# Feed-forward units whose output products come one unit later in a fused decoder trunk

## The reference

```python
for i in range(2):
    x = x + 0.5 * swiglu_ffn(rms_norm(x, ffn1_norm[i]), ffn1_w_in[i], ffn1_w_out[i])
    x = x + mixer_i(rms_norm(x, mix_norm[i]))     # i = 0: pooling + convolution; i = 1: spatial gating
    x = x + 0.5 * swiglu_ffn(rms_norm(x, ffn2_norm[i]), ffn2_w_in[i], ffn2_w_out[i])
return rms_norm(x, final_norm)

def swiglu_ffn(x, w_in, w_out):                   # w_in (1024, 5632), w_out (2816, 1024)
    gate, up = jnp.split(x @ w_in, 2, axis=-1)
    return (jax.nn.silu(gate) * up) @ w_out
```

## Time and profile before

| | |
|---|---|
| median of three runs | 899.32 us |
| the profiled execution's own time | 900.39 us |
| its span, first to last instruction | 898.6 us |
| mean granted TensorE clock | 0.996 |
| TensorE (PE) busy | 885.0 us |
| weight loads (PEld) busy | 737.6 us |
| VectorE (DVE) busy | 567.7 us |
| ScalarE (ACT) busy | 421.1 us |
| GpSimd (POOL) busy | 57.3 us |
| read from HBM | 168.11 MB |

### The profile page before, as it was taken

The page is one execution under the profiler, slowest core; times in us unless marked ns, Lnnn a source line. Parts: engine busy times, 40 slices in busy tenths (PEclk is TensorE's granted clock), DMA queues, the critical chain, the costliest instruction groups (busy, mean ns, idle before and its releaser), DMA issues.

```text
span 898.6 us, 11277 instructions
## 1 busy us (share of the span) xinstructions
PE 885.0 (98%) x4114; PEld 737.6 (82%) x4114; DVE 567.7 (63%) x595; ACT 421.1 (47%) x470; POOL 57.3 (6%) x60
## 2 busy tenths in 40 slices
PE   8899999999999999999999999999999999999997
PEld 7688888889888888888888888888899878888885
DVE  5666646757957765565566655665678476565653
ACT  7444435448845543444444534444553354443432
POOL 1000000404720000000000000000000000000000
PEclk9999999999999999999999999999999999999999
DMA  8885665643353877597638575675475278567531
GB/s 283 277 273 172 226 223 172 241 160 142 119 163 131 266 243 237 163 301 239 183 121 293 176 244 188 206 246 180 141 281 157 78 238 279 188 218 234 164 129 47
DMA packets 149933, 180.18 MB, mean 201 GB/s; under 512 B 7885, under 2 KB 134377, under 8 KB 149896
## 3 DMA queue, kind: packets, MB, share of 16 engines
q1 hardware_dynamic: 149880, 179.67, 60.9%
q10 hardware_dynamic: 16, 0.00, 0.0%
HBM read 168.11 MB, written 1.05 MB: 188 GB/s over the span
## 4 chain that ended last, share of the span: by engine, by line
PE 92%; DVE 2%; ACT 2%; DMA 2%; issue 1%; POOL 1%; SPq 1%; POOLq 0%; ACTq 0%
PE acc L1244 10%; PE acc L1246 10%; PE acc L1245 10%; PE ga L1244 10%; PE ga L1246 10%; PE ga L1245 10%; PE ub L1246 10%; PE ub L1245 10%; PE ub L1244 10%; PE tp L1306 1%; DMA xs<-xs 1%; DVE w_lo L866 1%; POOL w_lo L521 1%; DMA raw<-in_ffn_w_in_dram 0%; PE ga L1517 0%
## 5 line engine op out<-in xcount | busy, mean ns | idle before, releaser
L866 DVE TENSOR_TENSOR w_lo<-raw,w_hi 128x2048 fp32r<-128x2048 f32 x147 | 333.8, 2297 | 78.1 <-ACT w_hi L561 76.3
L561 ACT ACTIVATE w_hi<-raw 128x2048 fp32r<-128x2048 f32 x151 | 284.2, 1907 | 28.3 <-DMA raw<-in_ffn_w_in_dram 16.3
L1244 PE MATMUL acc<-w_hi,act_hi 128*128 128x512 f32 x416 | 164.3, 395 | 3.8 <-DVE act_lo L1042 3.8
L1246 PE MATMUL acc<-w_hi,act_lo 128*128 128x512 f32 x416 | 162.5, 391 | 0.0
L1245 PE MATMUL acc<-w_lo,act_hi 128*128 128x512 f32 x416 | 162.3, 390 | 0.0
L1244 PE MATMUL ga<-w_hi,xn_hi 128*128 128x512 f32 x384 | 150.8, 393 | 1.5 <-DVE w_lo L950 1.2
L1246 PE MATMUL ga<-w_hi,xn_lo 128*128 128x512 f32 x384 | 149.5, 389 | 0.0
L1244 PE MATMUL ub<-w_hi,xn_hi 128*128 128x512 f32 x384 | 149.5, 389 | 0.0
L1246 PE MATMUL ub<-w_hi,xn_lo 128*128 128x512 f32 x384 | 149.5, 389 | 0.0
L1245 PE MATMUL ga<-w_lo,xn_hi 128*128 128x512 f32 x384 | 149.4, 389 | 0.0
L1245 PE MATMUL ub<-w_lo,xn_hi 128*128 128x512 f32 x384 | 149.4, 389 | 0.0
(11 more groups left out here) (160 smaller groups left out, 652.0 us busy)
## 6 DMA issues: line engine op xcount, KB each, us to landing
raw<-in_ffn_w_in_dram SPq DMA_DIRECT2D x172, 512.0 KB, 4.9
raw<-in_ffn_w_out_dram SPq DMA_DIRECT2D x88, 512.0 KB, 4.2
xs<-xs SPq DMA_DIRECT2D x160, 64.0 KB, 2.1
raw<-in_sgu_w_in_dram SPq DMA_DIRECT2D x16, 512.0 KB, 4.9
raw<-in_ab_w_in_dram SPq DMA_DIRECT2D x12, 512.0 KB, 5.3
raw<-in_ab_w_out_dram SPq DMA_DIRECT2D x8, 512.0 KB, 4.1
raw<-in_sgu_w_out_dram SPq DMA_DIRECT2D x8, 512.0 KB, 5.7
raw<-in_ffn_w_in_dram SPq DMA_DIRECT2D x8, 256.0 KB, 5.9
```

The lines of the kernel that those rows point to most:

```text
L561: act.activation(w_hi[:, n % RING, :], raw[:, n % RAW, :], ACT.Copy).then_inc(hi_split, 1)
L866: dve.tensor_tensor(w_lo[:, n % RING, :], raw[:, n % RAW, :], w_hi[:, n % RING, :].bitcast(F32), ALU.subtract).then_inc(lo_split, 1)
L1244: pe.matmul(dst, s_hi, m_hi, start=start, stop=False)
L1246: return pe.matmul(dst, s_lo, m_hi, start=False, stop=stop)
```

## The change

Five things are edited.

1. On TensorE an FFN stage runs unit 0, unit 1, unit 2, output of unit 0, unit 3, output of unit 1, ... The outputs of units 8, 9 and 10 stand behind unit 10. The output slab of unit 0 is now slab b + 6; slabs b + 4 and b + 5 are unit 2's.
2. ScalarE, VectorE and SyncE follow that order. `hidden_hi` gets a wait for `slab_used`. `to_turn` of a stage's unit 9 moves from the next stage's first loads to behind its own last load.
3. `norm` on VectorE makes the low part of token tile 0's second half after the additions of token tile 1, and after mixer 1 two slabs are split inside `norm(k, 0)` (`ahead`).
4. `between` is called for each half of the output product, so that the transposes of half 1 come after three more matmuls.
5. Eight more warm-up matmuls, in three groups behind waits, follow the four.

```diff
 # SyncE
+                    for a in range(2):
+                        load_rows(b + 2 + a, w_in, a, pair(WIDTH, FF))
                     def turn(i, run):
                         for j in range(2):
-                            n, s = b + 2 + 3 * j, 1 + j
+                            n, s = b + 4 + 3 * j, 2 + j
                             for a in range(2):
                                 load_rows(n + a, w_in, a, pair(s * WIDTH, FF, i), run)
-                            if j or run is not None:
-                                to_turn(d + s - 1, run)
-                            load_out(n + 2, w_out, bass.ds(i * 4 + 2 * (s - 1), 2), run)
+                            to_turn(d + s - 1, run)
+                            load_out(n + 2, w_out, bass.ds(i * 4 + 2 * j, 2), run)
...
+                        load_rows(n + a, w_in, a, pair((STEPS - 1) * WIDTH, FF))
+                    to_turn(d + STEPS - 2)
                     for s in range(STEPS - 3, STEPS):
-                        if s == STEPS - 2:
-                            to_turn(d + STEPS - 2)
-                        load_out(n, w_out, slice(2 * s, 2 * s + 2))
-                        n += 1
-                    if k + 1 == len(stages):
-                        to_turn(d + TURNS)
+                        load_out(n + s - STEPS + 5, w_out, slice(2 * s, 2 * s + 2))
+                    to_turn(d + TURNS)
 # ScalarE
-            def norm(k, t):
+            def norm(k, t, ahead=0):
...
+                split_to(ahead)
...
-            def hidden_hi(slot, d, i=None):
+            def hidden_hi(slot, n, d, i=None):
+                act.wait_ge(slab_used, at(n, RING, i))
                 act.wait_ge(turn_landed, at(64 * d, 128, i))
...
                     split_to(b + 5)
+                    hidden_hi(0, b + 2, d + 1)
+                    split_to(b + 6)
+                    for t in range(TT):
+                        gate_rows(t, b + 2, r + 1, f + 1, ACT.Silu, scaled=late)
+                    split_to(b + 7)
                     with act.Fori(0, (STEPS - 3) // 2) as i:
                         for j in range(2):
-                            n, s = b + 2 + 3 * j, 1 + j
-                            hidden_hi(j, d + s, i)
+                            n, s = b + 4 + 3 * j, 2 + j
+                            hidden_hi(1 - j, n, d + s, i)
                             split(n + 4, i)
...
+                    n, s = b + 4 + 3 * (STEPS - 3), STEPS - 1
+                    hidden_hi(1, n, d + s)
+                    split_to(n + 4)
+                    for t in range(TT):
+                        gate_rows(t, n, r + s, f + s, ACT.Silu, scaled=late)
+                    last_hi(e // STEPS + 1)
+                    split_to(n + 7)
 # VectorE
+                if t:
+                    norm_lo(k, 0, 1)
                 dve.wait_ge(ms_ready, 4 * k + 2 * t + 2)
...
+                split_to(ahead)
+                norm_lo(k, t, 0)
+                if t:
+                    norm_lo(k, t, 1)
...
                     split_to(b + 5)
+                    hidden_lo(0, e)
+                    split_to(b + 6)
+                    for t in range(TT):
+                        product_rows(t, g + 2, scaled=late)
+                        to_blocks(t, f + 1)
+                    split_to(b + 7)
...
+                    n, s = b + 4 + 3 * (STEPS - 3), STEPS - 1
+                    hidden_lo(1, e + s - 1)
+                    split_to(n + 4)
+                    for t in range(TT):
+                        product_rows(t, g + 2 * s, scaled=late)
+                    last_lo(e + s)
+                    split_to(n + 7)
 # TensorE
             warm_up(WARM_UP)
+            pe.wait_ge(first_hi, 1)
+            warm_up(3)
+            pe.wait_ge(first_lo, 1)
+            warm_up(3)
+            pe.wait_ge(hi_piece, 1)
+            warm_up(2)
...
                     def step(j, start, i=None):
-                        n = b + 2 + 3 * j
-                        unit(n, f + 1 + j, i)
+                        n = b + 4 + 3 * j
+                        unit(n, f + 2 + j, i)
                         step_out(n + 2, j, e + 1 + j, start, i)
+                    unit(b + 2, f + 1)
                     step(0, True)
...
+                    unit(n, f + STEPS - 1)
                     slab_ready(out8)
                     pe.wait_ge(h_done, e + STEPS - 2)
                     slab_out(out8, 0, 0, False, False)
...
                     turned()
-                    slab_out(out8 + 1, 0, 2, False, False, parts=(1,))
-                    slab_out(out8, 1, 0, False, False, parts=(0,))
+                    slab_ready(out8 + 1)
+                    pe.wait_ge(h_done, e + STEPS - 1)
+                    slab_out(out8 + 1, 0, 2, False, False)
                     slab_ready(out8 + 2)
                     pe.wait_ge(h_done, e + STEPS)
                     slab_out(out8 + 2, 0, 4, False, True).then_inc(first_out, 1)
-                    slab_out(out8, 1, 0, False, False, parts=(1,)).then_inc(slab_used, 1)
+                    slab_out(out8, 1, 0, False, False).then_inc(slab_used, 1)
                     slab_out(out8 + 1, 1, 2, False, False).then_inc(slab_used, 1)
-                        slab_out(out8 + 2, 1, 4, False, True, lambda: transposes(k + 1, 0)).then_inc(slab_used, 1)
+                        slab_out(out8 + 2, 1, 4, False, True, lambda h: transposes(k + 1, 0, (h,))).then_inc(slab_used, 1)
```

More of the change, by code:

```diff
@@ L357, in _ @@
                 b, d = base[k], ffn0[k] // STEPS * TURNS
-                after = k > 0 and stages[k - 1][0] == "ffn"
                 if kind == "ffn":
@@ L405, in _ @@
                             .then_inc(mix1_landed, 16)
-                    n = b + 2 + 3 * (STEPS - 3)
+                    n = b + 4 + 3 * (STEPS - 3)
                     for a in range(2):
[L408 to L412, removed]
-                    for s in range(STEPS - 3, STEPS):
-                        if s == STEPS - 2:
-                            to_turn(d + STEPS - 2)
-                        load_out(n, w_out, slice(2 * s, 2 * s + 2))
-                        n += 1
-                    if k + 1 == len(stages):
-                        to_turn(d + TURNS)
+                        load_rows(n + a, w_in, a, pair((STEPS - 1) * WIDTH, FF))
+                    to_turn(d + STEPS - 2)
+                    for s in range(STEPS - 3, STEPS):
+                        load_out(n + s - STEPS + 5, w_out, slice(2 * s, 2 * s + 2))
+                    to_turn(d + TURNS)
                 elif kind == "mix0":
@@ L422, in _ @@
                     for j in range(2):
-                        if j:
-                            to_turn(d)
                         load_rows(b + j, ab_w_in[0], j, pair(gate, a - gate))
@@ L693, in _ @@
                 else:
-                    norm(k, 0)
+                    norm(k, 0, b + 3 if stages[k - 1][0] == "mix1" else 0)
                     split_to(b)
@@ L887, in root_wait, with norm_lo, norm @@
                 dve.wait_ge(rstd_ready, roots)
-            def norm(k, t):
+            def norm_lo(k, t, h):
+                n = small[("norm", k, t, h)]
+                dve.wait_ge(xn_hi_ready, 4 * (k - 1) + 2 * t + h + 1)
+                hi = xn_hi[:, 4 * h:4 * h + 4, t * P:(t + 1) * P]
+                dve.tensor_tensor(xn_lo[:, 4 * h:4 * h + 4, t * P:(t + 1) * P],
+                                  tp[n % 2][:, :].rearrange("p (c t) -> p c t", c=4),
+                                  hi.bitcast(F32), ALU.subtract).then_inc(small_free, 1)
+            def norm(k, t, ahead=0):
                 scale = 0.5 if stages[k - 1][0] == "ffn" else 1.0
@@ L1080, in _ @@
                     split_to(b + 5)
+                    hidden_lo(0, e)
[4 more added lines that the diff above has]
+                    split_to(b + 7)
                     with dve.Fori(0, (STEPS - 3) // 2) as i:
                         for j in range(2):
-                            n, s = b + 2 + 3 * j, 1 + j
-                            hidden_lo(j, e + j, i)
+                            n, s = b + 4 + 3 * j, 2 + j
+                            hidden_lo(1 - j, e + 1 + j, i)
                             split(n + 4, i)
@@ L1279, in slab_out @@
                 for c in parts:
-                    if between is not None and c == 1:
-                        between()
                     for h in range(2):
+                        if between is not None and c == 1:
+                            between(h)
                         o = slice(c * D + h * HALF, c * D + (h + 1) * HALF)
@@ L1416, in tail @@
                             if k + 1 < len(stages):
-                                between = lambda: transposes(k + 1, 0)
+                                between = lambda h: transposes(k + 1, 0, (h,))
                             else:
@@ L1474, in _ @@
                             .then_inc(small_full, 1)
-                    n = b + 2 + 3 * (STEPS - 3)
-                    out8 = n + 4
-                    unit(n, f + STEPS - 2)
```

(7 more changed lines are left out.)

7 lines of the change are left out of this document (1 added, 6 removed).

## The result

The changed kernel takes 919.96 us (median of four runs, 917.49 to 922.19) against 898.52 us for the kernel before on the same chip: the ratio is 1.0235, with a 95% interval of 1.0216 to 1.0255. It is 21 us slower. Forecast were 912.0 us and a range of 905 to 917: the direction and the places are right, the size is not.

What follows compares the result with a forecast made beforehand. TensorE was taken as the bound, busy 885.0 of 898.6 us. Removed waits -7.15, new waits +12.6, clock +4.5, stage ends +2.1 and opening +0.65 made +12.7 us: 912.0 us, range 905 to 917.

Steps and rivals of the forecast that it cites:

- The opposite sign: Rival: unit 2's bank `ga` is free in time, so the kernel gains, 894.9 us; chance 0.10, of which 0.05 below 894.8.
- The rival's condition: For `ga` free at unit 2: a chain from unit 0's blocks to the product of 9.1 us or less, not 11.7.
- Together 12.6 us: New TensorE waits at unit 2's start: 4.1, 3.3, 2.6 and 2.6 us in stages 0, 2, 3 and 5.
- 3 x 1.5 = 4.5 us: Clock falls behind the waits at unit 2: three at 1.5 us each; bounds none and four, 0 to 6.0.
- every wait lowers the clock: Rival: all four waits at unit 2 bring a clock fall, 913.5 us; chance 0.15.
- 0.98 us did not (7.74): In the opening of the kernel before, an idle of 0.98 us was read as bringing no clock fall.
- The end of a stage: Three splits instead of two ahead of `norm`: transposes wait 0.7 us at three stage ends, 2.1 us (0 to 3).
- The opening: Eight more warm-up matmuls at kernel start: first 128x512 matmul near 8.8 us, a delay of 0.65 us (0.3 to 1.2).
- What the change removes: Stage 0's wait 3.45 and slow stretch 1.5, stage 5's waits 1.2, slow transposes 1.0: together 7.15 us.

Runs made afterwards that it cites:

- gates_ahead: Changed kernel with both engines' splits of slab b + 6 moved behind unit 1's gates and products; 896.4 us, 0.9966 of the kernel before.
- order_alone: Changed order of units and outputs with both gates_and_tail edits, but norm, transposes and warm-up as in the kernel before; 894.65 us, 0.9964 of the kernel before.
- gates_and_tail: gates_ahead plus the next stage's first slab split ahead of unit 10's gates; 893.33 us, 0.9932 of the kernel before.
- norm_alone: Kernel before with only the change's norm, `ahead` and transposes by halves; 895.44 us, 0.9969 of the kernel before.
- warm_alone: Kernel before with only the eight more warm-up matmuls added; 898.80 us, 0.9998 of the kernel before.

## Why the prediction was right in place and wrong in size

- *The opposite sign was not in danger.* Unit 2 behind unit 1 waits for unit 1's product, because slab b + 6's split stands ahead of the gates and its load behind `to_turn`. gates_ahead shows it: with that order undone the kernel is 2.6% faster than changed. The rival's condition was too mild, though: a chain of 9.1 us frees the bank in time for stages 3 and 5 only; by the prediction's own distances stage 2 wants 8.4 and stage 0 7.9.
- *"Together 12.6 us"*, the waits at unit 2, was mis-sized: they measured 14.95. The chain from unit 0's blocks to the product was put at 11.7 us (12.0 in stage 0) and is 12.1, 12.9, 12.1 and 12.5 us in stages 2, 3, 5 and 0. The missing part is mostly in the issues: I took 2.9 us from the blocks to the slab's second DMA, and it is 3.2 (stage 5) to 3.9 us (stage 3, where the four turn DMAs take 3.20 us and not 2.49). The first of the slab's two DMAs takes 0.59 us behind the turn's, not the 0.4 I took from another place. Landing was 4.4 for 4.3, and the splits and the product were as forecast. TensorE adds about 0.15 us between product and first matmul, and each restart costs 0.16 us besides the idle (36.50 - 31.63 - 4.48 - 0.23). I counted the restart for the waits removed and left it out for the new ones, 0.65 us over the four.
- *"3 x 1.5 = 4.5 us"*, the clock, is the term that failed most, and its upper bound of 6.0 did not hold. Measured in the same way, the four slow stretches cost some 8.1 us. I had one low stretch in the trace and took its length as fixed; two of four were twice as long. The count of falls was forecast as three and was four, since each wait came out above 3.0 us. Here the rival "every wait lowers the clock" had the right count and still the wrong price. The Trainium skill's rule ("TensorE: Matmul & The Clock Gate", HAM oscillation), that each such wait makes the next stretch start at half rate, agrees with this trace: four of four, though in stage 3 the first matmuls still ran at the full level. The prediction's lower limit for a fall, "0.98 us did not (7.74)", was misread. The small matmuls ahead of that idle start 0.21 us apart, which is still the low level (0.11 is their distance at the full one, in the changed kernel from 7.2 us on), and the 128x512 matmuls behind it run at the full one: the level rose inside that idle, and nothing could fall there. The sum does not use it, and the 0.97 us wait of order_alone, at the full level, shows that such an idle brought no fall.
- *The end of a stage*, 0.7 us each, measured 0.65 (1.95 together against 2.1). The mechanism is shown by gates_and_tail. Mending it won more than the wait, 3.1 us against 1.95; in the two profiles it is 3.7 us, made of the opening's 0.9, the waits' 1.95, some 0.15 us of refill at each end, and a 0.2 us wait in mixer 1 that comes and goes between profiles; 0.2 us are left. By the profiles the third split costs some 2.4 us.
- *The opening*: the first 128x512 matmul starts at 8.54 us, where 8.8 was forecast, and the delay at the end of unit 1 is 0.34 us for 0.65. That the first comes so near is partly luck: in the nine profiles with these warm-up matmuls it lies between 7.45 and 8.84 us.
- *What the change removes*: stage 0's wait and slow stretch, stage 5's two waits and the slow transposes are all gone, as forecast. But 5 us of it is stage 0's, and that was one execution's value: norm_alone and warm_alone, with the same instructions there, wait 2.2 and 2.0 us. With the new order mended, the kernel wins 6.3 us where 7.15 - 0.65 was the forecast of the parts.

In sum: 14.95 - 12.6 = 2.35 for the waits, 8.1 - 4.5 = 3.6 for the clock, 0.65 for restarts, some 0.3 at the ends of stages (the refill of the waiting transposes, less what their waits fell short) and -0.3 in the opening are 6.6 us; between 12.7 forecast and 19.3 measured in the spans lie 6.6. That the two agree to the tenth is luck, since each term is known to 0.1 or 0.2 us only.

There was a shorter way that I did not take. The trace before shows when VectorE made unit 1's product of token tile 0 in stage 3: from 476.77 to 477.19, while the new order wants it done at 477.15. That one row shows that there was no room even before anything was moved.

## What to carry to other kernels

When two stages of a pipeline that share a buffer lose the work that stood between them, ask who frees the buffer and what is queued ahead of the freeing instruction on its engine; here a split of data that was needed 11 us later stood in front of a product that was needed at once. Where the next unit wants the bank at once, work that frees it goes ahead of work that only prepares data for later. A wait of some 3 us on TensorE should be priced with the slow stretch behind it, here 8.1 us on top of 14.95, and a single such stretch in a trace gives its price no upper bound.

## What the runs showed of the hardware

- These are counts in the profiles of this case, for idles between the opening and the last matmul; they are no rule. Idles of TensorE up to 1.6 us brought no fall of the clock in any profile here; idles of 2.0 to 2.7 us brought one in four cases (2.0, 2.3, 2.3, 2.7) and none in two (2.2, 2.55); all fifteen from 2.8 us on brought one. The low level lasted 3.4 us or 6.8 us.
- Useless matmuls in a wait can pay: 48 of them, 10.9 us of TensorE's time, made the changed kernel 6.3 us faster by the medians.
- The first DMA of a slab took 0.59 us to issue directly behind the four turn DMAs, in all eight such places of the changed kernel, and 0.35 us where at least 0.4 us lay between (four places).
